# Deep block products: high and low activation parts in one 512-column matmul, and two weight sums of each fold made on GpSimd

## The reference

```python
def swiglu(h, w_gate_up, w_down):
    gu = h @ w_gate_up
    g, u = gu[..., :D_FF], gu[..., D_FF:]
    return (jax.nn.silu(g) * u) @ w_down      # D_FF = 2816
```

## Time and profile before

| what | value |
|---|---|
| median of 3 runs | 1383.2 us (1382.34 to 1383.29) |
| the profiled execution's own time | 1381.23 us |
| its span, first to last instruction | 1379.5 us |
| PE busy | 1366.8 us, 99% |
| DVE busy | 981.9 us, 71% |
| ACT busy | 678.9 us, 49% |
| GpSimd (POOL) busy | 126.8 us, 9% |
| granted TensorE clock | 0.998 of full speed |

### The profile page before, as it was taken

The page is one execution under the profiler, slowest core; times in us unless marked ns, Lnnn a source line. Parts: engine busy times, 40 slices in busy tenths (PEclk is TensorE's granted clock), DMA queues, the critical chain, the costliest instruction groups (busy, mean ns, idle before and its releaser), DMA issues.

```text
span 1379.5 us, 22062 instructions
## 1 busy us (share of the span) xinstructions
PE 1366.8 (99%) x8608; PEld 1229.9 (89%) x8608; DVE 981.9 (71%) x1335; ACT 678.9 (49%) x1000; POOL 126.8 (9%) x113
## 2 busy tenths in 40 slices
PE   9999999999999999999999999999999999999997
PEld 8988888889999998998877788988888999998997
DVE  6656556469878879875578755755549888888955
...
GB/s 356 258 92 61 108 92 31 92 85 115 123 92 114 102 110 152 181 184 153 101 84 48 80 42 77 185 152 77 43 95 70 145 93 123 93 116 139 144 183 77
DMA packets 45886, 160.87 MB, mean 117 GB/s; under 512 B 5472, under 2 KB 5984, under 8 KB 45664
## 3 DMA queue, kind: packets, MB, share of 16 engines
...
## 4 chain that ended last, share of the span: by engine, by line
PE 89%; DMA 4%; DVE 3%; issue 3%; ACT 1%; POOL 0%; SPq 0%; POOLq 0%; ACTq 0%; DVEq 0%
PE acc L2281 15%; PE acc L2283 15%; PE acc L2282 15%; PE acc L2604 8%; PE acc L2605 8%; PE acc L2606 8%; PE acc L2329 3%; PE acc L2330 3%; PE acc L2331 3%; DMA memT<-in_weights 2%; DMA raw<-in_weights 2%; PE aux L2606 1%; PE aux L2605 1%; PE aux L2604 1%; PE aux L2655 1%
## 5 line engine op out<-in xcount | busy, mean ns | idle before, releaser
L1367 DVE TENSOR_TENSOR w_lo<-raw,w_hi 128x1024 fp32r<-128x1024 f32 (+1 forms) x149 | 181.4, 1218 | 98.3 <-ACT w_hi L691 97.8
L691 ACT ACTIVATE w_hi<-raw 128x1024 fp32r<-128x1024 f32 (+1 forms) x149 | 153.0, 1029 | 82.6 <-PE acc L2283 43.1
L2281 PE MATMUL acc<-u_hi,w_hi 128*128 128x512 f32 x352 | 138.7, 394 | 0.0
L2283 PE MATMUL acc<-u_hi,w_lo 128*128 128x512 f32 x352 | 137.2, 390 | 0.0
L2282 PE MATMUL acc<-u_lo,w_hi 128*128 128x512 f32 x352 | 137.1, 389 | 0.0
L2604 PE MATMUL acc<-b_hi,s_hi 128*128 128x256 f32 x432 | 122.4, 283 | 0.0
L2605 PE MATMUL acc<-b_lo,w_hi 128*128 128x256 f32 x432 | 122.3, 283 | 0.0
L2606 PE MATMUL acc<-b_hi,w_lo 128*128 128x256 f32 x432 | 122.2, 283 | 0.0
L2605 PE MATMUL acc<-b_lo,s_hi 128*128 128x256 f32 x432 | 122.2, 283 | 0.0
L2606 PE MATMUL acc<-b_hi,s_lo 128*128 128x256 f32 x432 | 122.2, 283 | 0.0
L2604 PE MATMUL acc<-b_hi,w_hi 128*128 128x256 f32 x432 | 122.2, 283 | 0.0
...
## 6 DMA issues: line engine op xcount, KB each, us to landing
raw<-in_weights SPq DMA_DIRECT2D x253, 512.0 KB, 3.3
memT<-in_weights POOLq DMA_DIRECT2D x16, 512.0 KB, 6.0
raw<-in_weights POOLq DMA_DIRECT2D x8, 512.0 KB, 5.4
hT<-in_x_t ACTq DMA_DIRECT2D x4, 512.0 KB, 7.8
x_tok<-in_x ACTq DMA_DIRECT2D x4, 512.0 KB, 5.3
...
mem_tok<-in_mem ACTq DMA_DIRECT2D x2, 512.0 KB, 5.8
...
```

What stands on the lines that cost most here:

```text
L691: act.activation(w_hi[:, s, c], raw[:, s, c], ACT.Copy).then_inc(hi_ready, 1)
L1367: dve.tensor_tensor(w_lo[:, s, c], raw[:, s, c], w_hi[:, s, c].bitcast(F32), ALU.subtract)\
L2281: pe.matmul(out, w_h, x_h, start=first, stop=False)
L2283: return pe.matmul(out, w_l, x_h, start=False, stop=last)
```

## The change

In a fold, the high and low parts of the activations of a product lie in one tile with two halves, and one 512-column matmul multiplies the high weights with both: the low part's product lands in the left half of a PSUM bank, the high part's in the right half. The third matmul (low weights, high activations, 256 columns) adds to the right half. A fold then has 112 matmuls in place of 168, and a result is the sum of the two halves: the copies and quarters are 512 wide, and each `fold_add` becomes two instructions, one for each half, the second waiting for the first.

For folds 1 to 3 the weight sums are made in another way. DVE makes `t_mid` first, as unit 7 (with unit 1 in it) + unit 4; GpSimd computes `t_pre` = `t_mid` - unit 1 (`pre_sum`) and `t_last` = `t_mid` + unit 2 (`last_sum`) with instructions of its own, and the two DMAs into `t_pre` are left out. Fold 0 keeps those DMAs and has `t_last` made on GpSimd. `pre_sum` and `last_sum` are now what raises `lo_ready` by two each; the low parts have a count of their own, `fold_lo`. `last_sum` waits for the third product of the fold before and for all four low parts of its own fold. GpSimd's list becomes: `pre_sum`(i), `last_sum`(i), `third_sum`(i+1), the squares. In DVE's list `fold_last` goes, and the low part of `t_pre` moves behind add 20, the low part of unit 4 behind add 12.

```diff
-        fold_hi = at("fold_hi", 56, [P, PLAIN_K, S], F32R)
+        fold_both = at("fold_both", 0, [P, 2, 28, S], F32R)
+        fb_both = at("fb_both", 88, [P, 2, 3, KT, S // 2], F32R)
         fb_f = at("fb_f", 88, [P, 3, KT, S // 2])
-        fb_lo = at("fb_lo", 88, [P, 3, KT, S // 2], F32R)
-        fb_hi = at("fb_hi", 112, [P, 3, KT, S // 2], F32R)
...
+        def fold_lo_at(layer, i, m):
+
+            return 4 * fold_number(layer, i) + FOLD_UNIT[m] + 1
+
+        def mid_at(layer, i):
+
+            return (FOLDS - 1) * layer + i
...
-        def fold_part(layer, i, m):
-            return fold_bank(layer, i, m)[:, 0:S // 2]
+        def fold_part(layer, i, m, e):
+
+            return fold_bank(layer, i, m)[:, half(e)]
+
+        def fold_moving(m, k):
+
+            if m in (7, 5, 6):
+                return fb_both[:, :, (7, 5, 6).index(m), k, :]
+            return fold_both[:, :, k + (0 if m in (1, 4) else KT), half(1 if m in (3, 4) else 0)]
+
+        def fold_tmp(layer, i, c):
+
+            if (layer, i) == (LAYERS - 1, FOLDS - 1):
+                return fold_sum_copy(c)
+            return tmp[:, 0 if c in (11, 21) else 1, :]
+
+        def fold_sum_copy(c):
+
+            return {11: tmp[:, 2, :], 21: tmp[:, 3, :], 22: rstd_row[:, :]}[c]
...
-                    if m == 5:
-                        act.wait_ge(pre_in, 32 * (fold_number(layer, i) + 1))
+                    if m == 6 and i:
+                        act.wait_ge(mid_ready, mid_at(layer, i))
+                    elif m == 5 and i == 0:
+                        act.wait_ge(pre_in, 32 * (layer + 1))
                     else:
-                        act.wait_ge(lo_ready, fold_unit(layer, i, 1 if m == 6 else 4) + 1)
+                        act.wait_ge(lo_ready, fold_unit(layer, i, 4 if m == 3 else 7) + 1)
...
-                    dst = {1: copy_1, 6: copy_u, 7: copy_7}[m]
-                    act.activation(dst, fold_part(layer, i, m), ACT.Copy).then_inc(fcopied, 1)
+                    dst = {1: tmp[:, 2, :], 6: tmp[:, 3, :], 7: rstd_row[:, :]}[m]
+                    act.activation(dst, fold_bank(layer, i, m)[:, :], ACT.Copy).then_inc(fcopied, 1)
...
-            def first_sum(layer, i):
-
-                n = fold_number(layer, i)
-                if n:
-                    pool.wait_ge(fslo_ready, fold_sums_at(layer, i, 5) - 3)
-                pool.dma_start(t_pre, d["weights"][fold_unit(layer, i, 7)]).then_inc(pre_in, 16)
-                pool.wait_ge(pre_in, 32 * n + 16)
-                pool.dma_start(t_pre, d["weights"][fold_unit(layer, i, 4)], accum_op=ALU.add).then_inc(pre_in, 16)
+            def first_sum(layer):
+
+                pool.dma_start(t_pre, d["weights"][fold_unit(layer, 0, 7)]).then_inc(pre_in, 16)
+                pool.wait_ge(pre_in, 32 * layer + 16)
+                pool.dma_start(t_pre, d["weights"][fold_unit(layer, 0, 4)], accum_op=ALU.add).then_inc(pre_in, 16)
+
+            def pre_sum(layer, i):
+
+                pool.wait_ge(mid_ready, mid_at(layer, i))
+                pool.wait_ge(fold_lo, fold_lo_at(layer, i, 7))
+                pool.wait_ge(fslo_ready, fold_sums_at(layer, i - 1, 5))
+                x = fold_unit(layer, i, 1)
+                pool.wait_ge(raw_in[x % RING], 16 * (x // RING + 1))
+                pool.tensor_tensor(t_pre, t_mid, raw[:, x % RING, :], ALU.subtract).then_inc(lo_ready, 2)
+
+            def last_sum(layer, i):
+
+                if i:
+                    pool.wait_ge(fold_done, fold_at(layer, i - 1, 3))
+                else:
+                    pool.wait_ge(acc_done, F_ACC[layer] + A_DN + KT)
+                x = fold_unit(layer, i, 2)
+                pool.wait_ge(lo_ready, x)
+                pool.wait_ge(fold_lo, fold_lo_at(layer, i, 4))
+                pool.wait_ge(raw_in[x % RING], 16 * (x // RING + 1))
+                pool.tensor_tensor(t_last[:, :], t_mid, raw[:, x % RING, :], ALU.add).then_inc(lo_ready, 2)
 
             def down_sums(layer):
 
                 norm = 3 * layer + 3
                 pool.wait_ge(prod_ready, PLAIN * (layer + 1))
-                first_sum(layer, 0)
+                if layer:
+                    pool.wait_ge(fslo_ready, fold_sums_at(layer - 1, FOLDS - 1, 5))
+                first_sum(layer)
                 third_sum(layer, 0)
+                last_sum(layer, 0)
+                third_sum(layer, 1)
                 for i in range(1, FOLDS):
-                    third_sum(layer, i)
-                    first_sum(layer, i)
-                    if i >= 2:
-                        add_squares(norm, 2 * i - 2, max(1, 2 * i - 4))
+                    pre_sum(layer, i)
+                    last_sum(layer, i)
+                    if i + 1 < FOLDS:
+                        third_sum(layer, i + 1)
+                    if i < FOLDS - 1:
+                        add_squares(norm, 2 * i, max(1, 2 * i - 2))
                 add_squares(norm, KT if layer == 0 else KT - 2, KT - 4)
...
-                def fold_lo_part(i, m, ready=0):
+                def fold_lo_part(i, m):
                     n = fold_unit(layer, i, m)
                     dve.wait_ge(hi_ready, n + 1)
                     ins = dve.tensor_tensor(w_lo[:, n % RING, :], raw[:, n % RING, :], w_hi[:, n % RING, :].bitcast(F32),
                                             ALU.subtract)
-                    if ready:
-                        ins.then_inc(lo_ready, ready)
-
-                def fold_mid(i, ready=2):
-
-                    dve.wait_ge(pre_in, 32 * (fold_number(layer, i) + 1))
-                    if fold_number(layer, i):
+                    ins.then_inc(fold_lo, 1)
+
+                def fold_mid(i):
+
+                    n = fold_number(layer, i)
+                    if n:
                         dve.wait_ge(fshi_ready, fold_sums_at(layer, i, 6) - 3)
-                    dve.tensor_tensor(t_mid, t_pre, raw[:, fold_unit(layer, i, 1) % RING, :], ALU.add).then_inc(lo_ready, ready)
-
-                def fold_last(i):
-
-                    if i:
-                        dve.wait_ge(fold_done, fold_at(layer, i - 1, 3))
+                    x, y, z = [fold_unit(layer, i, m) for m in (1, 7, 4)]
+                    if i == 0:
+                        dve.wait_ge(pre_in, 32 * (layer + 1))
+                        dve.tensor_tensor(t_mid, t_pre, raw[:, x % RING, :], ALU.add).then_inc(lo_ready, 2)
                     else:
-                        dve.wait_ge(acc_done, a0 + A_DN + KT)
-                    dve.wait_ge(lo_ready, fold_unit(layer, i, 1) + 1)
-                    dve.tensor_tensor(t_last[:, :], t_mid, raw[:, fold_unit(layer, i, 2) % RING, :], ALU.add)                        .then_inc(lo_ready, 2)
+                        dve.wait_ge(third_in, 16 * (n + 1))
+                        dve.wait_ge(raw_in[z % RING], 16 * (z // RING + 1))
+                        dve.tensor_tensor(t_mid, raw[:, y % RING, :], raw[:, z % RING, :], ALU.add).then_inc(mid_ready, 1)
 
...
-                    copy = {11: copy_1, 21: copy_u, 22: copy_7}[c]
-                    dve.tensor_tensor(tmp[:, c // 20, half(1 if c == 22 else 0)], fold_part(layer, i, m), copy, ALU.add)\
+                    if c == 21:
+                        dve.wait_ge(fold_added, folded(layer, i - 1) + 1)
+                    dve.tensor_tensor(fold_tmp(layer, i, c), fold_bank(layer, i, m)[:, :], fold_sum_copy(c), ALU.add)\
                         .then_inc(fquarter_ready, 1)
 
                 def fold_add(i, c):
 
-                    j = 2 * i + c // 20
-                    e = slice(0, S) if c == 20 else half(c % 10 - 1)
-                    if c == 32:
-                        j, e = 2 * i, half(1)
-                        dve.wait_ge(fold_done, fold_at(layer, i, 5))
-                        ins = dve.tensor_tensor(hT[:, j, e], hT[:, j, e], fold_part(layer, i, 5), ALU.add)
-                    elif c == 12:
-                        if (layer, i) == (LAYERS - 1, FOLDS - 1):
+                    j = 2 * i + (c in (20, 21, 22))
+                    e = slice(0, S) if c == 20 else half(0 if c in (11, 21) else 1)
+                    out, op = hT[:, j, e], ALU.add
+                    if c in (12, 32):
+                        if (layer, i) == (LAYERS - 1, FOLDS - 1) and c == 12:
                             dve.wait_ge(fold_added, folded(layer, i - 1) + 4)
-                        dve.wait_ge(fold_done, fold_at(layer, i, 3))
-                        ins = dve.tensor_tensor(hT[:, j, e], hT[:, j, e], fold_part(layer, i, 3), ALU.add)
-                    elif c == 11:
-                        dve.wait_ge(fquarter_ready, fold_quarter_at(layer, i, 11))
-                        dve.wait_ge(acc_drained, a0 + A_DN + KT)
-                        ins = dve.tensor_tensor(hT[:, j, e], hT[:, j, e], tmp[:, 0, e], ALU.add)
+                        m = 3 if c == 12 else 5
+                        dve.wait_ge(fold_done, fold_at(layer, i, m))
+                        parts = [fold_part(layer, i, m, h) for h in range(2)]
```

(37 more changed lines are left out.)

17 lines of the change are left out of this document (9 added, 8 removed).

## The result

The change made the kernel slower: 1423.7 us (median of 6 runs, 1422.3 to 1425.2) against 1383.2, a ratio of 1.029 [1.0277, 1.0304]. The forecast was 1407 in a range up to 1414: the sign was right, and the loss was 40 us instead of 24. The profiled execution took 1425.2 us.

The account below looks back on a forecast made before the run. PE bounds the kernel, busy 1366.8 of 1379.5 us; after the change the loop sets the pace. Layer 0 loses 10.8 and layer 1 14.1, +24.9 on 1381.2 gives 1406.1; the median is 2.0 higher, predicted 1407, range 1382 to 1414.

Parts of the forecast that it names:

- PE: Merged matmuls in the folds: a product takes 2.77 us instead of 2.88, 0.75 us a fold, 6.0 us in all.
- Prices: Instruction costs: quarter 0.65 us, ACT's 512-column copy 0.53 (duration 0.62), GpSimd's sum 2.35; DVE gains 2.5 a fold, loses 1.14.
- Fold 0: Layer 0: last_sum(0) ends at 11.45 us, m = 5 starts at 13.2, m = 3 at 19.3, fold ends at 22.1.
- The chain: Closed loop from one low part of unit 4 to the next: 20.7 us, 24.2 with port turns; PE needs 19.4.
- DMA 5.4: Term of the loop: third_sum's accumulating load takes 5.4 us from issue to landing, the earlier trace's median.
- a rival with 0.16: third_sum lands late beside SP's loads of units 2 and 4: 6.5 to 8 us, +4 to +10, 1411 to 1417; chance 0.16.
- the tail: Layer 1's last fold and after: PE's fifth transpose loses 3.8 us to a late first scaled tile; +4.0 us in all.
- The port: DVE and GpSimd take strict turns at SBUF: adds 1.14 and 2.35 us to the loop; quarters and add 12 don't wait.
- The free port: Rival: GpSimd and DVE don't take turns in these places, the loop is 20.7 us; +4.1, 1387 us; chance 0.19.
- the faster case: Rival: the loop fits under PE's pace, matmul gain stands and stalls on the squares go: 1375 us; chance 0.13.
- The loop's form: Order from last_sum through third_sum's load, low parts, quarters and adds back to last_sum sets the fold's pace, not PE.
- the waits for copy 6: PE waits before m = 5 for ACT's copy: 2.1 us in fold 0, 1.8 in fold 1, 0.95 in fold 3.

Follow-up runs that it names:

- merge_only: The kernel before with the merged matmul, wide copies and quarters and double additions, weight sums made as before: 1387.2 us, ratio 1.0034.
- copy_first: The change with t_pre and t_last on DVE, fold 1's t_pre behind t_mid, quarter 22 first in fold 0, copy 6 before t_last's high part: 1384.9 us.
- merge_fix: merge_only with earlier squares, a low-part count per product, fold_mid(1) behind unit 7's low part, and the last fold's add 12 moved ahead: 1384.5 us.
- all_dve: The change with t_pre and t_last of folds 1 to 3 on DVE, quarter 22 first in fold 0, layer 0's last add 12 earlier: 1396.7 us.
- last_dve: third_first with last_sum back on DVE, pre_sum staying on GpSimd: 1389.7 us, ratio 1.0061.
- before_fix2: The kernel before, without the merge, with the four wait removals of merge_fix: 1379.6 us, ratio 0.9979.
- late_loads: The change with the slots of units 2 and 4 set free only after third_sum has landed: 1414.3 us, ratio 1.0229.
- filler: The change with extra unused 512-column matmuls on PE in three waits of folds 1 and 2: 1424.3 us, ratio 1.031.
- sums_only: The kernel before with its three 256-column matmuls, and the weight sums, counts and orders of the change: 1405.8 us, ratio 1.017.
- third_first: The change with third_sum(i+1) issued ahead of last_sum(i) in GpSimd's list: 1398.3 us, ratio 1.0115.
- half_pre: The change with GpSimd's pre_sum made over half its columns only: 1417.0 us, ratio 1.0243.

## Why the prediction was wrong in its size, by its own steps

**PE: right in sign, too large.** In the change matmuls of 512 and 256 columns follow each other at 0.23 to 0.24 and 0.11 to 0.12 us:

```profile
564.12 0.40 PE L2703 MATMUL acc<-fold_both,t_hi 128*128 128x512 f32 x1
564.36 0.28 PE L2705 MATMUL acc<-fold_both,t_lo 128*128 128x256 f32 x1
564.47 0.40 PE L2703 MATMUL acc<-fold_both,t_hi 128*128 128x512 f32 x1
```

A product of sixteen takes 2.77 us, as forecast, in folds 2 and 3 of layer 0, but 2.83 in fold 0. In merge_only 48 of the 56 products take 2.83 or a little more, in copy_first 38, and fold 0 without a wait takes 19.8 us (merge_fix, copy_first and all_dve) where 19.4 was forecast and 20.15 is the fold before; 19.4 was seen in fold 2 of last_dve. At 2.83 a product the merge is worth 0.05 us, not 0.11, so the 6.0 us are some 3 to 4. What sets the one pace or the other stays open: behind some waits the pace changed from 2.83 to 2.77, behind others back. No run had the 6 us.

**Prices: right.** Quarter 0.60 to 0.72 between starts (0.65 taken), ACT's wide copy 0.57 long (0.62), GpSimd's sum 2.39 and 2.40 without a turn (2.35). DVE's 2.5 us more in a fold: copy_first has 27.2 us more than before_fix2 on the page (1012.3 against 985.1); less six `t_pre` of 1.14, 2.55 a fold.

**Fold 0: right to 0.1 us.** `last_sum`(0) ended 11.45 us in, m = 5 started at 13.2, m = 3 at 19.2, and the fold ended at 22.1; 11.45, 13.2, 19.3 and 22.1 were written.

**The chain: right; the DMA in it was the step that failed.** Starts of m = 3, in us from the start of fold 0 of layer 0:

| | fold 0 | fold 1 | fold 2 | fold 3 |
|---|---|---|---|---|
| forecast | 19.3 | 45.2 | 69.3 | 89.6 |
| the change | 19.2 | 48.6 | 74.8 | 97.2 |
| late_loads | 19.2 | 45.6 | 70.2 | 93.2 |

With the landing at 5.4 us the forecast holds to 0.9 us for two turns of the loop. The step that failed read "DMA 5.4", from the earlier trace rows; in the folds of the change it took 7.6 to 8.8 us. That median is of transfers that left in other company: in the kernel before SP's loads left 1.4 us or more behind `third_sum`, in the change 0.2 and 0.75 us. The text itself names the two loads that the same `last_sum` sets free, but only as a rival with 0.16. It was no rival but a certainty of this change, and belonged in the sum. And the trace before had its price. The second load of `first_sum` (L1279) also accumulates; in fold 0 it left at 550.82, between two loads of SP:

```profile
550.62 0.86 SPq L665 DMA_DIRECT2D raw<-in_weights  x2
```

```profile
DMA to landing us min/median/max: 5.4/5.4/8.0
```

The second view is of L1279 in the fold stage of layer 0: the 8.0 is the one of fold 0, and in layer 1 it is 8.3. The medians of the earlier trace rows hide it. The rival's price, "+4 to +10", covers the 8.4 measured, but its 1411 to 1417 doesn't reach 1423.7: the landing is about half of the miss, and the rest is in the rows below.

Two slips of the sum are small: 1406.1 and 2.0 are 1408.1, not 1407, and folds 0 to 2 of layer 1 took 62.3 us before, not 62.0.

**By stage** (us; the landing is in the first and fourth line of the change):

| stretch | before | forecast | the change | late_loads |
|---|---|---|---|---|
| layer 0, folds 0 to 2 | 61.6 | 72.1 | 79.0 | 74.6 |
| fold 3 | 20.2 | 20.3 | 21.1 | 21.5 |
| from there to the folds of layer 1 | 660.4 | 660.4 | 664.3 | 664.2 |
| layer 1, folds 0 to 2 | 62.3 | 72.1 | 81.8 | 73.1 |
| last fold and tail | 32.7 | 36.7 | 34.2 | 37.3 |

The landing takes 13 us of the folds, of which late_loads gives some back in its tail. *Left out altogether:* 3.9 us behind fold 3. There PE waits 2.0 us for the sums of squares, and the granted clock falls to 0.86 in the stretch; the additions for the last tile stand behind the next layer's low parts on DVE. merge_only has 1.5 us of that wait, so most of it comes with the merge; in merge_fix, with add 12 moved ahead, it is 0.5. *Also left out:* a wait of 1.4 us before m = 3 of fold 3, since two low parts for the next layer stand ahead of the quarters on DVE, behind `last_sum`(3) and in the way of two squares. *Too large for this kernel:* the tail, +4.0 forecast and +1.5 measured. PE's fifth transpose waited 1.6 us, not 3.8, since m = 3 of fold 2 was so late that DVE and GpSimd had run ahead: the first scaled tile came 10.5 us into the fold. In late_loads it came at 13.4, as written, and the tail is 4.6 us longer than before. So the tail's reasoning held, and its miss follows from the landing.

**The port: right in kind.** Beside `pre_sum` DVE's subtraction took 3.26, beside `last_sum` GpSimd took 3.1. That quarters, which read PSUM and one SBUF tile, do not wait held: 0.68 beside GpSimd's sum in the change, and at most 0.69 in every run. Additions of a quarter to `hT` read two SBUF tiles, and beside GpSimd they waited: 0.69 became 2.46 in fold 1 of the change (add 20), and 0.42 became 1.71 in filler (add 11):

```profile
556.38 1.71 DVE L1936 TENSOR_TENSOR hT<-hT,tmp 128x256 f32<-128x256 f32 x1
```

No run had add 12 beside a sum on GpSimd.

**The clock: not foreseen,** and mostly hidden here, by the estimate from filler.

**The free port and the faster case** are refuted; sums_only's and third_first's costs show the loop, the 3.26 us beside `pre_sum` and half_pre the port. The loop's form was reasoned and held, but that 1407 was not further off owes something to errors of opposite sign: the waits for copy 6 in folds 1 and 3 of layer 0, forecast at 1.8 and 0.95 us, did not come, and the tail was shorter.
